# Two chained transformer blocks on one core: how the first unit starts, and four small orders in the second block

## The chip, the cores and the metric

The kernel runs on one core of a Trainium2 chip. The metric is the time of one execution on the device in microseconds (us); lower is better. The engines are TensorE (PE, with PEld for its weight loads), VectorE (DVE), ScalarE (ACT), GpSimd (POOL) and SyncE (SP), which here only issues DMAs.

## The reference

256 tokens of 1024 features go through a first block of two layers and then through a second block of two layers, all in float32. Cut to what matters here:

```python
def hybrid_layer(x, ...):            # first block, twice
    h = rms_norm(x, norm_mix_w)
    z = h @ w_in + b_in              # first unit: the first 512 columns
    ...                              # dilated attention, mLSTM, gates
    x = x + mixed @ w_out
    return x + jnp.square(relu(rms_norm(x, norm_mlp_w) @ w_ff1)) @ w_ff2

def first_block(x, ...):
    for l in range(2): x = hybrid_layer(x, ...)
    return rms_norm(x, final_norm_w)

def second_block(x, ...):            # again two layers
    for l in range(2):
        x = x + 0.5 * rmsnorm(swiglu_ffn(rmsnorm(x, pre_g), w_gu, w_down), post_g)
        x = x + rmsnorm(mixing_sublayer(rmsnorm(x, mix_pre_g), ...), mix_post_g)
        x = x + 0.5 * rmsnorm(swiglu_ffn(rmsnorm(x, pre2_g), w_gu2, w_down2), post2_g)
    return x
```

The mixing sublayer has four branches: a gated MLP, a pooling mixer, a sparse attention with a softmax, and a convolution of 31 taps.

## The kernel before

**Weights.** All weights come as chunks of 1 MB (128 partitions by 2048 floats, `CH` = 2048) in the order in which TensorE uses them, into three slots (`SLOTS` = 3). SP issues their DMAs, each after the slot's last low part is made (`lo_ready`). Each chunk is split: ScalarE writes `w_hi`, the chunk rounded to the matmul's format (`split_high`, L175), and VectorE writes `w_lo` = raw − `w_hi` (`split_low`, L182). The activations are split in the same way into `aH` and `aL`. A product is three matmuls: high·high, low·high, high·low. So TensorE does, for each chunk, one phase that needs `w_hi` and one that needs `w_lo` (for example L245 and then L251, or L327, L328 and then L335).

**Order.** Each engine runs a list in program order. `Splitter.upto(c)` puts the splits of all chunks up to `c` at that place of the list of ScalarE (`high`) or VectorE (`low`), so the lists interleave the splits with the rest of the work, written out by hand. Semaphores join the lists.

**The start (`first_block`).** SP issues: a head of constants with the identity (68 KB), token rows 0 to 127 (`x`, 512 KB), two halves of the first chunk, token rows 128 to 255, two halves of the second chunk, the third chunk. TensorE runs `WARM` = 4 matmuls on ones (L1313), transposes the first token tile (L1321), runs `FILL` = 3 matmuls on ones (L1360), then the first two products, and then the transposes of the second token tile. ScalarE and VectorE take the transposed tiles from the PSUM, times the norm's gain, into `aH` (`x_part_high`, L705) and `aL` (`x_part_low`, L931), and split the first two chunks in pieces (L719, L724, L726; L946, L959). `first_chunk` does the first unit of 512 columns with 48 matmuls, all of its products for one token tile before those for the other. Two `square_sum` (L411) on ScalarE give each token's sum of squares, from which VectorE makes `rstd`; the result is multiplied by it only when it is taken out of the PSUM (L994). GpSimd's list begins with two DMA issues, the broadcast rows `rows_a` (L617) and the constants (L619), once the second chunk has landed.

**The second block's start (layer 0).** VectorE multiplies each token tile by the final gain (L2366), then makes `first_v` and waits for its root from GpSimd. ScalarE squares the two new tiles (L2087), then makes the high part of chunk `F0[0] + 2`, the third that the feed-forward uses.

**`mlp`, four times.** VectorE makes the low parts of chunks 3 and 4 of the feed-forward one after the other, then `unit(1)` begins: the sum of halves of a (L262), its scaling (L2319), the sum of halves of b (L262 again), the low part of `lows[0]`, the product of both.

**The softmax, twice.** The rows of query tile 1 are normalised (L2532), then the low part of chunk `M0 + 17` is made, then query tile 0 is normalised (L2532). TensorE transposes the results (L2821, L2825).

Of the kernel before, what the change touches and what calls it, by code (L numbers as in the profile page):

```python
# [51 lines left out]
WARM, FILL = 4, 3  # L52
# [361 lines left out]
def token_rstd(k, dve, ch, layer, n):  # L414

    dve.wait_ge(k.ss_ready.sem, k.ss_ready.at(layer, TT * (n + 1)))
    dve.tensor_scalar(k.var[:, 0:TT], k.ss[:, 0:TT], 0.5 / DM, 0.5 * EPS, ALU.mult, ALU.add).then_inc(ch.sem, ch.one())
# [48 lines left out]
def first_block(nc, k, d, sems, block):  # L466

    with ExitStack() as ctx:
# [3 lines left out]
        def sig(name, per, start=0):  # L472
# [17 lines left out]
        R3 = sb("R3", [P, 8 * (SEQ + CONV - 1)])  # L490
        qk_tok = R1[:, 0:TT * 2 * AH * AD].rearrange("p (t h d) -> p t h d", t=TT, h=2 * AH)
# [59 lines left out]
        k.nT_done, k.aH_ready, k.a_ready = sig("nT_done", 8, 4), sig("aH_ready", 6, 4), sig("a_ready", 8, 4)  # L551
# [3 lines left out]
        x0_loaded, x1_loaded, half0_loaded, half1_loaded = (  # L555
            sig("x0_loaded", 0), sig("x1_loaded", 0), sig("half0_loaded", 0), sig("half1_loaded", 0))
        part_high, part_low = sig("part_high", 0), sig("part_low", 0)
        X_PARTS = tuple((tt, b) for tt in range(TT) for b in range(4))
        x_tile = lambda tt, kt: k.ps[:, ((4, 5, 6, 7), (2, 3, 4, 5))[tt][kt // 2], (kt % 2) * P:(kt % 2 + 1) * P]
# [55 lines left out]
        def _(pool):  # L615
            pool.wait_ge(k.raw_loaded[AHEAD_HIGH - 1], 16)
# [59 lines left out]
        def _(sp):  # L676
            sp.dma_start(consts[:, 0:KA_ADD], d.consts_a[:, 0:KA_ADD]).then_inc(head_loaded.sem, 16)
            sp.dma_start(k.x[:, 0, :], d.x[0:P, :]).then_inc(x0_loaded.sem, 16)
            sp.dma_start(k.raw[:, 0, 0:CH // 2], d.w_a[0, :, 0:CH // 2]).then_inc(half0_loaded.sem, 16)
            sp.dma_start(k.raw[:, 0, CH // 2:CH], d.w_a[0, :, CH // 2:CH]).then_inc(k.raw_loaded[0], 16)  # L680
            sp.dma_start(k.x[:, 1, :], d.x[P:2 * P, :]).then_inc(x1_loaded.sem, 16)
            sp.dma_start(k.raw[:, 1, 0:CH // 2], d.w_a[1, :, 0:CH // 2]).then_inc(half1_loaded.sem, 16)
# [11 lines left out]
        def _(act):  # L694
# [6 lines left out]
            def x_part_high(tt, b):  # L701

                act.wait_ge(k.nT_done.sem, 4 * tt + b + 1)
                for kt in (2 * b, 2 * b + 1):
                    ins = act.activation(k.aH[:, kt, tt * P:(tt + 1) * P], x_tile(tt, kt), ACT.Copy,  # L705
                                         scale=par[:, PA_NORM + kt:PA_NORM + kt + 1])
                ins.then_inc(k.aH_ready.sem, 1)

            def first_high():

                act.wait_ge(par0_loaded.sem, 16)
                for tt, b in X_PARTS[:2]:
                    x_part_high(tt, b)
                act.wait_ge(half0_loaded.sem, 16)
                for kt in range(4):
                    if kt == 2:
                        act.wait_ge(k.raw_loaded[0], 16)
                    cols = slice(kt * CH // 4, (kt + 1) * CH // 4)
                    act.activation(k.w_hi[0][:, cols], k.raw[:, 0, cols], ACT.Copy)\  # L719
                       .then_inc(part_high.sem if kt < 3 else k.hi_ready, 1)  # L720
                for tt, b in X_PARTS[2:]:
                    x_part_high(tt, b)
                act.wait_ge(half1_loaded.sem, 16)
                act.activation(k.w_hi[1][:, 0:CH // 2], k.raw[:, 1, 0:CH // 2], ACT.Copy).then_inc(part_high.sem, 1)  # L724
# [3 lines left out]
            for l in range(DEPTH):  # L728
# [7 lines left out]
                high.upto(2)  # L736
# [6 lines left out]
                if l == 0:  # L743
                    square_sum(k, act, l, 0, 0, junk)
                square_sum(k, act, l, 0, 1, junk)
# [144 lines left out]
        def _(dve):  # L890
# [6 lines left out]
            def angles(ch):  # L897

                dve.wait_ge(head_loaded.sem, 16)
# [26 lines left out]
            def x_part_low(tt, b):  # L926

                dve.wait_ge(k.aH_ready.sem, X_PARTS.index((tt, b)) + 1)
                for kt in (2 * b, 2 * b + 1):
                    cols = slice(tt * P, (tt + 1) * P)  # L930
                    ins = dve.scalar_tensor_tensor(k.aL[:, kt, cols], x_tile(tt, kt), par[:, PA_NORM + kt:PA_NORM + kt + 1],  # L931
                                                   k.aH[:, kt, cols].bitcast(F32), ALU.mult, ALU.subtract)
                ins.then_inc(k.a_ready.sem, 1)

            def first_low():

                dve.wait_ge(par0_loaded.sem, 16)
# [691 lines left out]
def second_block(nc, k, d, sems, block):  # L1629


    with ExitStack() as ctx:
# [581 lines left out]
        def _(dve):  # L2214
# [139 lines left out]
            for l in range(DEPTH):  # L2354
# [825 lines left out]
```

## Time and profile before

| | |
|---|---|
| median of 3 runs | 1792.0 us (1789.89 to 1793.45) |
| the profiled execution's own time | 1792.04 us |
| its span in the profile | 1790.3 us |
| mean granted clock of TensorE | 0.999 of full speed |

The span is the time between the first and the last recorded event of the core; some 1.7 us of the execution's time lie outside it. The profile comes from one execution. Its page gives busy times by engine; the timeline gives instructions by start and duration, neighbours of the same form in one row with a count (x8), and in brackets how long the engine had been idle and which event released it. A matmul of 512 columns is recorded with 0.38 us but such rows start 0.216 us apart, since matmuls are pipelined.

### The profile page before, as it was taken

To read this page: it belongs to the slowest core of one execution; us is meant where nothing else is said; L and a number is where in the kernel's file an instruction comes from. 1 tells how busy PE (TensorE), PEld (TensorE's weight loads), DVE (VectorE), ACT (ScalarE), POOL (GpSimd) and SP (SyncE) were. 2 spreads that over 40 slices of the span, in tenths; PEclk is the share of its full clock that TensorE was granted. 3 is DMA by queue.
4 is the path that set the end of the run, shared out by engine and by line. 5 is a ranking of instruction groups with operands and counts; after the bars stand their busy time and mean duration, and the time that the engine had idled before them with its cause. 6 is when DMAs were issued, how large, how long until landed. Compare 5 with 4: busy or idle time off the path is not lost.

```text
span 1790.3 us, 25922 instructions
## 1 busy us (share of the span) xinstructions
PE 1778.8 (99%) x10010; PEld 1588.6 (89%) x10010; DVE 1402.9 (78%) x1599; ACT 904.5 (51%) x998; POOL 219.7 (12%) x189
## 2 busy tenths in 40 slices
PE   9999999999999999999999999999999999999998
PEld 7988998889889898899898888998899898888997
DVE  7897867678869667777779987778777779987776
ACT  5564434445644444644555546444544555546443
POOL 0000000000001000000059230000000058230000
PEclk9999999999999999999999999999999999999999
DMA  9546565555556555655564556555655564555553
GB/s 315 205 157 227 188 212 209 189 215 200 187 215 222 205 196 186 214 197 194 181 204 172 183 210 217 202 196 192 223 199 197 188 203 167 186 212 205 201 197 117
DMA packets 52018, 357.43 MB, mean 200 GB/s; under 512 B 6552, under 2 KB 6688, under 8 KB 10080
## 3 DMA queue, kind: packets, MB, share of 16 engines
q1 hardware_dynamic: 47952, 341.93, 54.1%
q0 software_dynamic: 3696, 14.33, 2.7%
q8 instruction: 57, 0.93, 0.2%
q14 instruction: 25, 0.20, 0.0%
q10 hardware_dynamic: 288, 0.04, 0.0%
HBM read 354.15 MB, written 2.11 MB: 199 GB/s over the span
## 4 chain that ended last, share of the span: by engine, by line
PE 94%; DVE 4%; issue 1%; ACT 1%; DMA 1%; DVEq 0%; POOLq 0%; POOL 0%; SPq 0%; ACTq 0%
PE ps L245 21%; PE ps L327 13%; PE ps L335 13%; PE ps L328 13%; PE ps L251 11%; PE ps L207 3%; PE ps L208 3%; PE ps L209 3%; PE ps L225 2%; PE ps L232 2%; PE ps L226 2%; DVE w_lo L182 1%; PE ps L2917 1%; PE ps L2916 1%; PE ps L2921 1%
## 5 line engine op out<-in xcount | busy, mean ns | idle before, releaser
L182 DVE TENSOR_TENSOR w_lo<-raw,w_hi 128x2048 fp32r<-128x2048 f32 x312 | 717.4, 2305 | 208.4 <-ACT w_hi L175 208.0
L175 ACT ACTIVATE w_hi<-raw 128x2048 fp32r<-128x2048 f32 x312 | 596.1, 1912 | 424.1 <-PE ps L335 168.6
L245 PE MATMUL ps<-a,w_hi 128*128 128x512 f32 x1760 | 398.3, 379 | 0.8 <-ACT w_hi L175 0.8
L245 PEld LDWEIGHTS ps<-a,w_hi 128*128 128x128 f32 x1760 | 329.3, 189 | 46.0 <-ACT w_hi L175 1.2
L327 PE MATMUL ps<-w_hi,a 128*128 128x512 f32 x592 | 226.9, 383 | 0.0
L328 PE MATMUL ps<-w_hi,a 128*128 128x512 f32 x592 | 224.4, 379 | 0.0
L251 PEld LDWEIGHTS ps<-a,w_lo 128*128 128x128 f32 x1760 | 213.6, 192 | 5.9
L327 PE MATMUL ps<-w_hi,mix 128*128 128x512 f32 x576 | 218.7, 380 | 0.0
L328 PE MATMUL ps<-w_hi,mix 128*128 128x512 f32 x576 | 218.3, 379 | 0.0
L251 PE MATMUL ps<-a,w_lo 128*128 128x256 f32 x1760 | 214.2, 275 | 0.0
L335 PE MATMUL ps<-w_lo,a 128*128 128x512 f32 x592 | 139.8, 379 | 0.0
L335 PE MATMUL ps<-w_lo,mix 128*128 128x512 f32 x576 | 136.1, 379 | 0.0
L262 DVE TENSOR_REDUCE GU<-ps 128x512 f32<-128x1024 f32 x80 | 97.9, 1223 | 44.0 <-PE ps L251 44.0
L327 PEld LDWEIGHTS ps<-w_hi,a 128*128 128x128 f32 x592 | 111.9, 189 | 17.3 <-issue 1.4
L335 PEld LDWEIGHTS ps<-w_lo,a 128*128 128x128 f32 x592 | 111.9, 189 | 15.9
L328 PEld LDWEIGHTS ps<-w_hi,a 128*128 128x128 f32 x592 | 111.9, 189 | 15.1
L335 PEld LDWEIGHTS ps<-w_lo,mix 128*128 128x128 f32 x576 | 108.9, 189 | 15.4
L328 PEld LDWEIGHTS ps<-w_hi,mix 128*128 128x128 f32 x576 | 109.1, 189 | 13.7
L327 PEld LDWEIGHTS ps<-w_hi,mix 128*128 128x128 f32 x576 | 109.1, 189 | 13.6
L2041 ACT ACTIVATE GU<-GU 128x512 f32<-128x512 f32 x36 | 22.6, 629 | 176.1 <-DVE GU L2319 176.1
L1859 POOL TENSOR_TENSOR pss<-pss,neg_half 128x1 f32<-128x1 f32 x12 | 6.7, 558 | 690.8 <-DVE pss L2243 690.8
L225 PE MATMUL ps<-a,w_hi 128*128 128x256 f32 x320 | 73.2, 277 | 0.0
(416 smaller groups left out, 2267.2 us busy)
## 6 DMA issues: line engine op xcount, KB each, us to landing
raw<-in_w_b SPq DMA_DIRECT2D x198, 1024.0 KB, 4.9
raw<-in_w_a SPq DMA_DIRECT2D x124, 1024.0 KB, 4.9
rows<-in_post_gains POOLq DMA_DIRECT2D x6, 512.0 KB, 5.9
rows<-in_rows_a POOLq DMA_DIRECT2D x2, 1028.0 KB, 8.3
raw<-in_w_a SPq DMA_DIRECT2D x4, 512.0 KB, 7.1
rows<-in_rows_a POOLq DMA_DIRECT2D x2, 1024.0 KB, 6.9
x<-in_x SPq DMA_DIRECT2D x2, 512.0 KB, 6.0
a_gates<-bias_line POOLq DMA_DIRECT2D x2, 512.0 KB, 7.7
```

The costliest lines, as they stand in the source:

```text
L175: act.activation(k.w_hi[s], k.raw[:, s, :], ACT.Copy).then_inc(k.hi_ready, 1)
L182: dve.tensor_tensor(k.w_lo[s], k.raw[:, s, :], k.w_hi[s].bitcast(F32), ALU.subtract).then_inc(k.lo_ready, 1)
L207: pe.matmul(out, a[0], hi, start=first, stop=False)
L208: pe.matmul(out, a[0], lo, start=False, stop=False)
L209: return pe.matmul(out, a[1], hi, start=False, stop=end)
L225: pe.matmul(out, w, halves_in_turn(act(kt)[0]), start=n == 0 and kt == kts[0], stop=False)
L245: pe.matmul(both, hi[:, kt, n * P:(n + 1) * P], k.a[:, :, kt, :].rearrange("p s (t n) -> p s n t", t=TT), start=kt == 0, stop=False)
L251: end = pe.matmul(high, lo[:, kt, n * P:(n + 1) * P], halves_in_turn(k.aH[:, kt, :]), start=False, stop=kt == KT - 1)
L262: return dve.tensor_reduce(dst.rearrange("p f (t n) -> p f n t", t=TT), k.ps[:, bank:bank + 2, :].rearrange("p b (s n t) -> p b n t s", s= ...
L327: pe.matmul(in_pairs(out(tt, h)), a[0], w, start=first and i == 0, stop=False)
L328: pe.matmul(in_pairs(out(tt, h)), a[1], w, start=False, stop=False)
L335: ins = pe.matmul(in_pairs(out(tt, h)), act(kt)[0][:, tt * P:(tt + 1) * P], halves_in_turn(lo[:, i, h * step:(h + 1) * step]), start=False ...
```

## The change

1. **Tokens by features.** A new input `x_t` holds the tokens as features by tokens. SP loads it in four pieces of 256 KB between pieces of the first two chunks; it lies in `R1`. The 16 transposes, the two sets of `x_part_high` and `x_part_low` and `FILL` are gone, `WARM` is 8. ScalarE makes `aH` with `x_high(kt)` (256 columns from SBUF), interleaved with quarters of the chunks; VectorE makes `aL` with `x_low(kt)` (256 columns, both inputs in SBUF), interleaved with `quarter_low` and `next_low` (six pieces of 512 columns, one of 1024).
2. **Squares.** GpSimd squares each piece and adds it up, 15 operations of 128x256, ahead of its DMA issues. TensorE sums over the partitions with two matmuls by a column of ones after the first unit; `token_rstd` reads the PSUM. The two `square_sum` of layer 0 are gone.
3. **`first_chunk`** goes by `kt`: for both token tiles high·high, then low·high, then high·low, each after its own piece.
4. **Token rows** (`x`, 2 × 512 KB) are loaded by SP behind chunks 3 to 5; VectorE waits for them (`x_loaded`) ahead of the first residual that needs them.
5. **Second block, layer 0, start:** on ScalarE `high.upto(F0[0] + 2)` now stands ahead of the two squares; on VectorE `first_v` comes before the second gain multiply, and `low.upto(2)` before the wait for the root.
6. **`mlp`:** the low part of chunk 4 moves from behind that of chunk 3 to behind the sum of halves of b in `unit(1)`, in all four.
7. **Softmax:** the low part of chunk `M0 + 17` moves from between the two normalisations to behind both, in both layers.

```diff
-WARM, FILL = 4, 3
+WARM = 8
...
+            for kt in range(KT):
+                if kt == 0:
+                    pool.wait_ge(xT01_loaded.sem, 16)
...
+                if kt > 1:
+                    pool.wait_ge(squares.sem, 2 * kt - 1)
+                pool.tensor_tensor(xx[:, min(kt, 1), :], xT[:, kt, :], xT[:, kt, :], ALU.mult).then_inc(squares.sem, 1)
+                if kt > 0:
+                    pool.wait_ge(squares.sem, 2 * kt)
+                    pool.tensor_tensor(xx[:, 0, :], xx[:, 0, :], xx[:, 1, :], ALU.add).then_inc(squares.sem, 1)
             pool.wait_ge(k.raw_loaded[AHEAD_HIGH - 1], 16)
...
+            sp.dma_start(xT[:, 0:2, :], x_t[:, 0:2, :]).then_inc(xT01_loaded.sem, 16)
...
-            with sp.Fori(1, DEPTH * CA // SLOTS) as g:
+            for s in range(SLOTS):
+                sp.wait_ge(k.lo_ready, s + 1)
+                sp.dma_start(k.raw[:, s, :], d.w_a[SLOTS + s]).then_inc(k.raw_loaded[s], 16)
+            for tt in range(TT):
+                sp.dma_start(k.x[:, tt, :], d.x[tt * P:(tt + 1) * P, :]).then_inc(x_loaded.sem, 16)
+            with sp.Fori(2, DEPTH * CA // SLOTS) as g:
...
+            def x_low(kt):
+
+                dve.wait_ge(k.aH_ready.sem, kt + 1)
+                dve.scalar_tensor_tensor(k.aL[:, kt, :], xT[:, kt, :], par[:, PA_NORM + kt:PA_NORM + kt + 1],
+                                         k.aH[:, kt, :].bitcast(F32), ALU.mult, ALU.subtract).then_inc(k.a_ready.sem, 1)
...
+                x_low(0)
+                quarter_low(0)
...
+                x_low(6)
+                x_low(7)
+                next_low(2, CH // 2, CH)
...
+                for i in range(4):
+                    kt = 4 * half + i
...
+                    pe.wait_ge(k.aH_ready.sem, kt + 1)
...
+                            if half == 1:
+                                pe.wait_ge(squares.sem, 2 * KT - 1)
+                                for tt in range(TT):
+                                    ins = pe.matmul(k.ps[:, 6, tt:tt + 1], xx[:, 0, tt * P:(tt + 1) * P], ones[:, 0:1], start=True, stop=True)
+                                ins.then_inc(k.ss_ready.sem, TT)
...
                 if l == 0:
+                    high.upto(F0[0] + 2)
                     for tt in range(TT):
...
                 split_low(k, dve, st, l, F0[f] + 3)
-                split_low(k, dve, st, l, F0[f] + 4)
...
                     if j == 1:
+                        split_low(k, dve, st, l, F0[f] + 4)
                         split_low(k, dve, st, l, lows[0], trips)
...
                     dve.memset(v_tok[:, :, :, BD:BD + 1], 1.0).then_inc(vone_ready.sem, 1)
+                    low.upto(2)
                     dve.wait_ge(first_root.sem, 1)
...
                 for qt, cols in ((1, slice(P, 3 * P)), (0, slice(0, P))):
-                    if qt == 0:
-                        low.upto(M0 + 17)
...
                     dve.tensor_tensor(v, v, last(rsum[:, qt, :], (1 + qt) * P), ALU.mult).then_inc(p_ready.sem, 1)
+                low.upto(M0 + 17)
```

## Rows read from the trace of the kernel before

**Rows 1.** The page: busy time of each engine, its share of the span, instructions.

```profile
PE 1778.8 (99%) x10010; PEld 1588.6 (89%) x10010; DVE 1402.9 (78%) x1599; ACT 904.5 (51%) x998; POOL 219.7 (12%) x189
```

**Rows 2.** TensorE's waits: engine line waited for: total, times, longest.

```profile
PE ps L1321 <- DMA x<-in_x: 1.2, 1, 1.2
PE ps L2825 <- DVE RL L2532: 0.9, 1, 0.9
```

**Rows 3.** Timeline of TensorE, 0 to 33 us: start, duration, instruction, wait.

```profile
1.26 3.78 PE L1313 MATMUL ps<-ones 128*128 128x256 f32 x8 [1.26 <-DVE mv_tok L895]
...
7.15 1.46 PE L1360 MATMUL ps<-ones 128*128 128x256 f32 x6
9.37 0.45 PE L207 MATMUL ps<-w_hi,a 128*128 128x512 f32 x1 [0.75 <-DVE w_lo L946]
9.66 0.38 PE L208 MATMUL ps<-w_lo,a 128*128 128x512 f32 x1
...
20.93 0.38 PE L327 MATMUL ps<-w_hi,a 128*128 128x512 f32 x1
```

**Rows 4.** Timeline of VectorE, 8 to 26 us.

```profile
8.54 2.49 DVE L946 TENSOR_TENSOR w_lo<-raw,w_hi 128x512 fp32r<-128x512 f32 x4
...
14.30 2.36 DVE L959 TENSOR_TENSOR w_lo<-raw,w_hi 128x1024 fp32r<-128x1024 f32 x2 [0.17 <-ACT w_hi L724]
...
24.68 1.40 DVE L994 SCALAR_TENSOR_TENSOR R<-ps,rstd,rows 128x512 f32<-128x512 f32 x2
```

**Rows 5.** Windows: engines' busy us (instructions), clock, DMA share, GB/s.

```profile
2.00:4.00 2.00, 2.00 (x7) 1.56 (x6) 0.00 (x0) 1.23 (x2) 0.00 (x0) 1.00 0.90 202
4.00:6.00 2.00, 1.04 (x3) 0.32 (x1) 0.00 (x0) 0.00 (x0) 0.00 (x0) 1.00 1.03 346
```

**Rows 6.** Timeline of VectorE, 724 to 1011 us: forms alone, beside GpSimd.

```profile
724.72 4.49 DVE L182 TENSOR_TENSOR w_lo<-raw,w_hi 128x2048 fp32r<-128x2048 f32 x2 [0.50 <-ACT w_hi L175]
...
929.93 2.11 DVE L2439 SCALAR_TENSOR_TENSOR conv_y<-conv_x,rows,conv_y 128x256 f32<-128x256 f32 x4
...
983.59 4.04 DVE L2439 SCALAR_TENSOR_TENSOR conv_y<-conv_x,rows,conv_y 128x256 f32<-128x256 f32 x10
...
1005.71 5.39 DVE L182 TENSOR_TENSOR w_lo<-raw,w_hi 128x2048 fp32r<-128x2048 f32 x2
```

**Rows 7.** Timeline of GpSimd, 1004 to 1012 us.

```profile
1004.77 0.63 POOL L1916 TENSOR_TENSOR sum<-sum 128x265 f32<-128x265 f32 x1
...
1006.29 2.66 POOL L1916 TENSOR_TENSOR sum<-sum 128x257 f32<-128x257 f32 x1
1009.03 2.66 POOL L1930 TENSOR_TENSOR pooled<-sum,consts 64x256 f32<-64x256 f32 x1
```

**Rows 8.** The page's DMA issues: count, KB each, us from issue to landing.

```profile
rows<-in_rows_a POOLq DMA_DIRECT2D x2, 1028.0 KB, 8.3
```

**Rows 9.** Timeline of all engines, 717 to 721 us: the second block begins.

```profile
717.79 1.06 ACT L2087 ACTIVATE b_qkF<-x 128x1024 f32<-128x1024 f32 x1 [0.26 <-DVE x L2366]
...
718.84 1.89 ACT L175 ACTIVATE w_hi<-raw 128x2048 fp32r<-128x2048 f32 x1
...
720.79 3.72 PE L245 MATMUL ps<-a,w_hi 128*128 128x512 f32 x16 [0.79 <-ACT w_hi L175]
```

**Rows 10.** Timeline of all engines, 732 to 736 us: a feed-forward's second unit.

```profile
732.45 1.23 DVE L262 TENSOR_REDUCE GU<-ps 128x512 f32<-128x1024 f32 x1 [0.61 <-PE ps L251]
...
733.60 2.28 DVE L182 TENSOR_TENSOR w_lo<-raw,w_hi 128x2048 fp32r<-128x2048 f32 x1
...
735.71 1.46 PE L335 MATMUL ps<-w_lo,mix 128*128 128x512 f32 x6
```

**Rows 11.** Timeline of VectorE and TensorE, 978 to 984 us: the softmax's end.

```profile
978.81 3.36 DVE L182 TENSOR_TENSOR w_lo<-raw,w_hi 128x2048 fp32r<-128x2048 f32 x1
...
983.73 0.65 PE L2825 MATMUL ps<-consts,RL 128*128 128x128 f32 x4 [0.93 <-DVE RL L2532]
```

**Rows 12.** The chain of waits, 937 to 1017 us: start, us, what.

```profile
1015.95 1.16 PE ps L2844 x8
```

More of the change, by code:

```diff
@@ L411, in square_sum, with token_rstd @@
     act.activation(junk[:, tt, :], k.x[:, tt, :], ACT.Square, accum_out=k.ss[:, tt:tt + 1]).then_inc(k.ss_ready.sem, 1)
-def token_rstd(k, dve, ch, layer, n):
+def token_rstd(k, dve, ch, layer, n, sums=None):
     dve.wait_ge(k.ss_ready.sem, k.ss_ready.at(layer, TT * (n + 1)))
-    dve.tensor_scalar(k.var[:, 0:TT], k.ss[:, 0:TT], 0.5 / DM, 0.5 * EPS, ALU.mult, ALU.add).then_inc(ch.sem, ch.one())
+    dve.tensor_scalar(k.var[:, 0:TT], k.ss[:, 0:TT] if sums is None else sums, 0.5 / DM, 0.5 * EPS, ALU.mult, ALU.add).then_inc(ch.sem, ch.one())
     dve.wait_ge(ch.sem, ch.at(layer))
@@ L676, in _ @@
         def _(sp):
[L677 to L682 removed]
+            quarter = CH // 4
@@ L699, in _, with x_high @@
             act.activation(first_use[:, :], ones[:, 0:1], ACT.Copy)
[L701 to L707, printed above, removed]
+            def x_high(kt):
+                if kt < 2:
+                    act.wait_ge(xT01_loaded.sem, 16)
+                elif kt < 4:
+                    act.wait_ge(kt2_loaded.sem, 2 * 16)
+                elif kt < 6:
+                    act.wait_ge(half1_loaded.sem, 2 * 16)
+                else:
+                    act.wait_ge(head_loaded.sem, 2 * 16)
+                act.activation(k.aH[:, kt, :], xT[:, kt, :], ACT.Copy, scale=par[:, PA_NORM + kt:PA_NORM + kt + 1])\
+                   .then_inc(k.aH_ready.sem, 1)
@@ new lines, in quarter_high @@
+            def quarter_high(q):
+                if q == 0:
+                    act.wait_ge(quarter0_loaded.sem, 16)
+                elif q == 1:
+                    act.wait_ge(quarter1_loaded.sem, 16)
+                elif q == 2:
+                    act.wait_ge(kt2_loaded.sem, 2 * 16)
+                else:
+                    act.wait_ge(k.raw_loaded[0], 16)
+                cols = slice(q * CH // 4, (q + 1) * CH // 4)
+                act.activation(k.w_hi[0][:, cols], k.raw[:, 0, cols], ACT.Copy)\
+                   .then_inc(part_high.sem if q < 3 else k.hi_ready, 1)
@@ L709, in first_high @@
             def first_high():
                 act.wait_ge(par0_loaded.sem, 16)
[L712 to L724, printed above, removed]
+                x_high(0)
+                quarter_high(0)
+                x_high(1)
+                quarter_high(1)
+                x_high(2)
+                quarter_high(2)
+                x_high(3)
+                quarter_high(3)
+                x_high(4)
@@ L725, in first_high @@
+                act.activation(k.w_hi[1][:, 0:CH // 4], k.raw[:, 1, 0:CH // 4], ACT.Copy).then_inc(part_high.sem, 1)
+                x_high(5)
+                act.activation(k.w_hi[1][:, CH // 4:CH // 2], k.raw[:, 1, CH // 4:CH // 2], ACT.Copy).then_inc(part_high.sem, 1)
+                x_high(6)
+                x_high(7)
                 act.wait_ge(k.raw_loaded[1], 16)
@@ L735, in _ @@
                     high_of(k, act, l, 0, par[:, PA_NORM:PA_MLP], k.aH)
-                high.upto(2)
+                high.upto(3 if l == 0 else 2)
                 if l == 1:
@@ L1355, in x_next @@
                         ins.then_inc(qkT_done.sem, 1)
-            pe.wait_ge(head_loaded.sem, 16)
-            x_transpose(0)
-            for _ in range(FILL):
-                pe.matmul(k.ps[:, 1, 0:SEQ], ones[:, 0:P], ones[:, :], start=True, stop=True)
             for l in range(DEPTH):
```

144 lines of the change are left out of this document (79 added, 65 removed).

## The prediction

> **What bounds the kernel now.** I read the busy line of the page first: TensorE is busy 1778.8 of the span's 1790.3 us [rows 1]. So only TensorE's own waits can be won. Its list of waits names the places [rows 2]: 1.2 us for the first token tile and 0.9 us for the softmax's second normalisation, and the timeline has 0.79 at the second block's start [rows 9]. The timeline of the first microseconds adds what no list of waits shows: work that isn't the product. TensorE warms up from 1.26, runs fill at 7.15, starts the first product at 9.37 and the second unit at 20.93 [rows 3]. The mark for the prologue is that 20.93: behind it TensorE runs on the stream of chunks. A change anywhere else counts only if it moves the start of a matmul, so for each of the later edits I read the timeline of all engines around it.
>
> **Prologue, if nothing but TensorE bounds it.** Eight warm matmuls make 16 records. The first 8 took 3.78 us from 1.26; those at full pace took 1.46 for 6 [rows 3], of which the pace is 0.216, so 8 more take 1.7: warm ends at about 6.7. The first piece of tokens is by then in: the core's DMAs move 202 GB/s from 2 to 4 us and 346 from 4 to 6 [rows 5], so 256 KB land at about 4.2 and the next 256 KB, the first quarter of the chunk, at 4.9. The 48 matmuls at 0.216 take 10.37, the two sums over partitions 0.24: 17.35 instead of 20.93, a gain of 3.6. That is the case in which VectorE keeps up.
>
> **VectorE in the prologue.** The pieces of the low parts are priced by rows: 512 columns 0.60 each (2.49 for 4), 1024 columns 1.15 (2.36 for 2) [rows 4], 256 columns with both inputs in SBUF 0.40 (4.04 for 10) [rows 6]. Eight, six and one of them: 3.20 + 3.60 + 1.15 = 7.95 us. Alone they would follow ScalarE's pieces and end early enough.
>
> **GpSimd beside it.** GpSimd is at rest there before; now it runs 15 operations of 128x256, 14 of them beside VectorE's. What that costs is the largest unknown. Two low parts of 2048 columns take 4.49 us alone (at 724.72) and 5.39 (at 1005.71) beside GpSimd [rows 6], while GpSimd's operation of 128x257 takes 2.66 instead of the 0.63 of the like one at 1004.77 [rows 7]: it stands until VectorE's is through, and then VectorE's next one stands for it. The two alternate one by one: GpSimd's two stretched operations start 2.74 apart (1006.29 and 1009.03) [rows 7], and between them lies one low part, whose pace alone is 2.20 (4.49 less the last one's 2.29). So one GpSimd operation with two inputs costs VectorE 0.54. The bounds: below, nothing, as in the paragraph on TensorE, or the 0.2 that two GpSimd operations with one input each cost the four operations of 256 columns at 929.93 (2.11 where the ten at 983.59 give 4 × 0.40 and a tail of 0.07) [rows 6]; above, 0.68, a little over GpSimd's own 0.63 [rows 7], since its operation can't block for longer than it lasts with its start. The case in hand has two inputs and the same 256 columns, so I take 0.54: 14 × 0.54 = 7.56 us. VectorE starts with the first piece at 4.9 and ends its last at 4.9 + 7.95 + 7.56 = 20.4. Behind that piece stand 8 matmuls, 1.73, and the sums: 22.4 against 20.93, **+1.5 us**. With 0.2 each VectorE ends at 4.9 + 7.95 + 2.8 = 15.7 and TensorE at 17.6: −3.3, and −2.9 with some waits for pieces. With 0.68 each it ends at 22.4: +3.5.
>
> The row shows GpSimd's operation lengthened from 0.63 to 2.66 and VectorE's pair by 0.90. The Trainium skill, "SBUF — State Buffer", section "Who interferes with whom", says that the two share a port pair as an exclusive lock for a whole instruction, where VectorE has two SBUF inputs and GpSimd reads SBUF; PE and ACT have ports of their own. By that rule taken strictly each GpSimd operation costs its full length of 0.63: 14 × 0.63 is 8.8 us, 1.3 above the 7.56, and the prologue would lose 2.7 instead of 1.5. The trace agrees with the exclusive turns and shows a little less than the full length.
>
> **Transfers and what waits behind.** GpSimd issues the broadcast rows at about 19.4 to 21 instead of 13.12. They take 8.3 us to land [rows 8], so they are there at 27.7 to 29.3; VectorE takes the first unit out at 24.68 before [rows 4], then at 27.8 to 29.4 and is done 1.40 later. TensorE overwrites those banks with the third unit, 10.4 after the second's start, so at 32.8: 2 us are left, cost 0. The token rows' 1 MB delays the chunks behind it by at most the 3.0 us that 1 MB takes at 346 GB/s [rows 5]; three slots of chunks, 5.2 us of TensorE each, cover that: 0. ScalarE is freed of two square sums, which no matmul waited for: 0. The late wait for `x` stands near the end of the first layer: 0.
>
> **Second block's start.** TensorE's phase at 720.79 waited 0.79 for ScalarE's high part, made at 718.84 behind the second square at 717.79 [rows 9]; the lost time against the pace is 0.95. With the high part ahead of two squares of 1.06 it starts at about 716.4 and is ready at 718.3, and VectorE's low part, now ahead of the wait for the root, at 720.7: **−0.95**. The squares come 1.7 later, so `Silu` and the two high parts behind it by about 1.2; the first of those is then ready at 725.85, for a phase that would start 5.2 behind this one, at 726: nothing to spare, so −0.6 to −1.0.
>
> **Low part in `mlp`.** The sum of halves ends and the low part stands at 733.60, 2.28 long, so to 735.88; TensorE's low phase of chunk 4 starts at 735.71 [rows 10]. Before, chunk 4's low part was made at about 726.9, the second of the pair at 724.72 [rows 6], and the place at 733.60 held chunk 5's. Moved there it is seen by TensorE at about 735.94: 0.23 late, and a phase that had to stop starts with a step of 0.29 instead of 0.216, as 9.37 to 9.66 [rows 3]. 0.32 for each of the four feed-forwards (the other three show the same three rows, with the low phase 3.26 behind the sum in each): **+1.3** (0 to +1.4; VectorE idled 0.61 to 1.49 before that sum [rows 10], which may let it start sooner).
>
> **Low part in the softmax.** TensorE stands 0.93 at 983.73 for the second normalisation, which stood behind the low part of 3.36 at 978.81 [rows 11]. Moved behind, that wait goes, 1.1 with the restart. But the chain of waits from there to 1015.95 runs through VectorE [rows 12], whose work up to there is the same in sum; what TensorE gains at 983.73 it waits at L2844 for: **0** (−1.1 to +0.3). In layer 1 no wait stands there.
>
> **Sum.** +1.5 − 0.95 + 1.3 + 0 = +1.85 on the profiled execution's 1792.04, which is the median of the three runs (1792.0): **1793.9 us**. The bounds of the terms give 1792.04 − 3.6 − 1.0 + 0 − 1.1 = 1786.3 and 1792.04 + 3.5 − 0.6 + 1.4 + 0.3 = 1796.6.
>
> **Rivals.**
> 1. *GpSimd's squares stay off VectorE's way* (the cost is 0.2 or less). For: with one input the row shows so little [rows 6], and the operations have gaps between them, in which GpSimd waits for its own result. Against: the row with two inputs. Then −3.6 to −2.9 in the prologue: 1792.04 − 3.3 − 0.95 + 1.3 = 1789.1, and 1787.8 if the move in `mlp` is free too, 1786.7 if the softmax pays as well. Chance 0.32. One of those two extras is needed to get below 1788.4; I give that 0.55 of it.
> 2. *Slower: the broadcast rows come too late.* GpSimd's chain waits for data, for VectorE and for itself; if its last operation ends past 23.2, the rows land past 31.5 and VectorE empties the banks past 32.9. From that point each microsecond is one of TensorE's: an end at 27 (15 operations of 1.5) gives +3.8 more, 1797.7. For: GpSimd's operations beside VectorE took 2.66 each [rows 7]. Against: those stood behind low parts of 2.2, here behind 0.4 to 0.6. Chance 0.12.
> 3. *Slower: the clock.* Now TensorE waits for each piece, and the granted clock could fall; the rows at half pace took 0.43 for what takes 0.216 [rows 3]. Ten matmuls at that pace cost 2.2: 1796.1. Against: in 4 to 6 us, with 1.04 of 2.00 busy, the clock stays 1.00 [rows 5]. Chance 0.06.
> 4. *The softmax's move pays* the 1.1 us, with the rest as forecast: 1792.8; or the move in `mlp` costs nothing: 1792.6. Within the forecast's own range.
>
> **How the numbers follow.** The forecast has 0.50 and its own range 1791 to 1796. What a measurement of this kernel can tell from no change is 0.2%, 3.6 us: below 1788.4 is faster, above 1795.6 slower. Faster has 0.55 of rival 1, 0.18, and 0.02 of the forecast: 0.20. Slower has rivals 2 and 3 with 0.18, of which 0.03 stay inside and as much comes from the forecast's upper end: 0.18. The rest, 0.62, is the same. The range is 1786.7 to 1797: the first rival down to both extras and the upper bound of the terms; what is left out is most of rival 2 (0.1) and the tail below.
>
> **What would show it.** The second unit's first matmul at 22.4 (17.4 in rival 1). VectorE's pieces of 256 columns one by one at 0.9 to 1.0 of spacing, alternating with GpSimd's; GpSimd's 15 operations ending at 19 to 21. No wait at the phase at 720.79; a wait of 0.2 us at the low phase L335 in each feed-forward; no wait at L2825 but one of about 1 us at L2844. The prediction is wrong if VectorE's pieces keep their 0.4 and 0.6 us beside GpSimd, or if a new wait at the first evictions appears.

## The result and the profile after

The changed kernel takes 1794.12 us (median of 18 runs, 1792.88 to 1797.16) against 1791.43 us (18 runs, 1789.89 to 1793.45): a ratio of 1.0017 with the 95% interval 1.001 to 1.0024 (the medians themselves give 1.0015). That is 2.7 us slower, clear of no change, inside the 0.2% that were called the same (the interval's upper end is just outside), and 0.2 us from the forecast of 1793.9. The change itself was forecast at +1.85, from a profile of before that was 0.6 above the median of its 18 runs, so the two totals are closer than the two differences. The profiled execution of the changed kernel was its fastest, 1792.88 us with a span of 1791.2 us, so I took a second profile (experiment 1) before reading anything off the first.

TensorE's waits on the page of after: total, times, longest.

```profile
PE ps L1398 <- DVE w_lo L996: 2.0, 2, 1.6
PE ps L1387 <- ACT w_hi L768: 1.1, 1, 1.1
PE ps L1398 <- DVE w_lo L986: 0.3, 1, 0.3
```

They all lie in the prologue. The two of the second block [rows 2, 9, 11] are gone. TensorE in the prologue and at the three later places:

```profile
12.27 0.70 PE L1398 MATMUL ps<-w_lo,a 128*128 128x512 f32 x2 [0.33 <-DVE w_lo L986]
...
14.12 0.67 PE L1387 MATMUL ps<-w_hi,a 128*128 128x512 f32 x2 [1.15 <-ACT w_hi L768]
...
20.25 0.70 PE L1398 MATMUL ps<-w_lo,a 128*128 128x512 f32 x2 [1.62 <-DVE w_lo L996]
...
22.44 0.46 PE L327 MATMUL ps<-w_hi,a 128*128 128x512 f32 x1
...
721.87 3.62 PE L245 MATMUL ps<-a,w_hi 128*128 128x512 f32 x16
...
736.91 1.99 PE L335 MATMUL ps<-w_lo,mix 128*128 128x512 f32 x8
...
983.93 0.60 PE L2884 MATMUL ps<-consts,RL 128*128 128x128 f32 x4
...
1015.88 1.16 PE L2903 MATMUL ps<-consts,y 128*128 128x128 f32 x8
```

The second unit starts at 22.44 against 20.93 [rows 3]: +1.5, and 22.4 was forecast. The way there is another than the sum said. VectorE, its share of it:

```profile
5.50 0.79 DVE L976 SCALAR_TENSOR_TENSOR a<-R,a_par,a 128x256 fp32r<-128x256 f32 x1 [4.25 <-ACT a L739]
6.22 1.22 DVE L986 TENSOR_TENSOR w_lo<-raw,w_hi 128x512 fp32r<-128x512 f32 x1
...
13.49 0.48 DVE L976 SCALAR_TENSOR_TENSOR a<-R,a_par,a 128x256 fp32r<-128x256 f32 x1 [1.27 <-ACT a L739]
14.01 1.10 DVE L996 TENSOR_TENSOR w_lo<-raw,w_hi 128x512 fp32r<-128x512 f32 x1
15.04 0.83 DVE L976 SCALAR_TENSOR_TENSOR a<-R,a_par,a 128x256 fp32r<-128x256 f32 x1
15.79 1.22 DVE L996 TENSOR_TENSOR w_lo<-raw,w_hi 128x512 fp32r<-128x512 f32 x1
16.93 1.71 DVE L976 SCALAR_TENSOR_TENSOR a<-R,a_par,a 128x256 fp32r<-128x256 f32 x2
18.56 1.63 DVE L996 TENSOR_TENSOR w_lo<-raw,w_hi 128x1024 fp32r<-128x1024 f32 x1
```

GpSimd beside it, and the end of its chain:

```profile
15.66 0.80 POOL L631 TENSOR_TENSOR R<-R 128x256 f32<-128x256 f32 x1
16.61 0.88 POOL L628 TENSOR_TENSOR R<-R 128x256 f32<-128x256 f32 x1
...
19.19 1.59 POOL L631 TENSOR_TENSOR R<-R 128x256 f32<-128x256 f32 x1
20.73 0.74 POOL L633 DMA_DIRECT2D rows<-in_rows_a  x1
```

A piece of 256 columns that takes 0.40 alone is followed 0.75 later by the next (15.04 to 15.79), one of 512 columns 1.14 later (15.79 to 16.93) instead of 0.60. From 5.50 to the end of the last piece (the next instruction starts at 20.11) are 14.6 us, of which 1.27 is a gap ahead of 13.49; the pieces alone are 7.95, so GpSimd's 14 operations cost 5.4, 0.39 each, not 0.54 (0.41 if the one at 12.99, which ran in the gap, isn't counted). The gap and a start 0.6 late make up for it. The start: ScalarE's first piece waited for the constants with the norm's gain (`a_par`) until 4.96, and VectorE's stands 0.5 behind it, a step that the sum left out. The gap comes from the transfers, in the windows of after (busy times of PE, PEld, DVE, ACT, POOL; clock; share and GB/s of the DMAs) and in ScalarE's timeline:

```profile
4.00:6.00 2.00, 2.00 (x9) 1.69 (x8) 0.50 (x1) 1.00 (x2) 1.17 (x2) 1.00 0.97 277
6.00:8.00 2.00, 2.00 (x10) 1.54 (x9) 2.00 (x4) 1.31 (x4) 0.91 (x3) 1.00 1.02 355
8.00:10.00 2.00, 2.00 (x11) 1.70 (x9) 2.00 (x3) 1.84 (x4) 1.84 (x3) 1.00 1.00 252
18.00:20.00 2.00, 0.63 (x3) 0.20 (x2) 2.00 (x2) 1.48 (x2) 1.84 (x3) 1.00 0.08 33
```

```profile
12.95 0.51 ACT L739 ACTIVATE a<-R,a_par 128x256 fp32r<-128x256 f32 x1 [2.86 <-DMA raw<-in_w_a]
```

From 4 to 10 us the DMAs move 277, 355 and 252 GB/s, where before they moved 346 [rows 5] and then 379 and 410, and ScalarE starts on the fifth piece of tokens only at 12.95. What released it there is not the tokens. The kernel lets the fifth and sixth piece wait for two transfers with one semaphore (`half1_loaded`): the tokens, issued at 3.62 and landed 6.6 later, at 10.2, and the first half of the second chunk, issued at 4.14 and landed 8.8 later, at 12.9. With a semaphore of their own the two token pieces, and GpSimd's squares of them, could have run in the gap; no run tried it. TensorE's clock stays at 1.00.

**Where the time goes.** TensorE runs the same list in all kernels from the second unit on, so I matched its matmuls one by one and took, for each profile, the start of a matmul less its start in the profile of before. The offsets in us (the first column is the start of the second unit, the others stand just behind the places named; in the last column the end):

| profile | 20.9 | 120 | 719, ahead of the second block | 731 | 737, first low phase | 1017, behind the softmax | 1275 | 1560 | end |
|---|---|---|---|---|---|---|---|---|---|
| after | 1.51 | 2.03 | 2.03 | 0.98 | 1.30 | −0.07 | 0.60 | 0.50 | 0.83 |
| 1 after again | 1.65 | 4.22 | 4.21 | 3.15 | 3.48 | 3.01 | 3.67 | 4.57 | 4.89 |
| 2 prologue only | 1.25 | 2.47 | 2.47 | 2.45 | 2.45 | 1.22 | 1.22 | 2.10 | 2.10 |
| 3 second block only | −0.50 | −0.51 | −0.51 | −1.56 | −1.23 | −1.80 | −1.14 | −0.83 | −0.49 |
| 4 one square | −1.25 | 2.52 | 2.52 | 1.49 | 1.82 | 0.48 | 1.16 | 2.53 | 2.87 |
| 5 rows later | 1.16 | 1.24 | 1.24 | 0.21 | 0.54 | 0.51 | 1.19 | 1.22 | 1.56 |
| 6 rows later, one square | −1.39 | −1.10 | −1.10 | −2.14 | −1.81 | −2.33 | −1.65 | −0.18 | 0.17 |
| 7 low part 4 back | 1.13 | 1.49 | 1.49 | 0.46 | 1.64 | 0.57 | 0.60 | 0.95 | 0.96 |
| 8 orders, no low part 4 | −0.56 | −0.60 | −0.60 | −1.67 | −0.49 | −0.99 | −0.98 | −1.00 | −1.00 |
| 9 orders, first low part 4 | −0.70 | −0.71 | −0.71 | −1.78 | −1.46 | −2.85 | −2.85 | −2.52 | −2.52 |

Their ends agree with the executions' own times: 1792.04 + 0.83 = 1792.87 for 1792.88, 1792.04 + 4.89 = 1796.93 for 1796.94. Each row is one execution: that of 3 was the fastest of its 11 runs, those of 4 and 6 the slowest of theirs, so the last column isn't the medians' order.

### The profile page after: what moved, and what is told of

The parts are those of the page before. It is cut to its first block, busy times and chain, and to the rows that moved or that the text cites. A ratio compares the mean times of both kernels' runs of the same rounds, so it can differ in the third digit from the quotient of the medians.

```text
span 1791.2 us, 25902 instructions
## 1 busy us (share of the span) xinstructions
PE 1779.5 (99%) x10000; PEld 1587.3 (89%) x10000; DVE 1407.9 (79%) x1592; ACT 900.6 (50%) x987; POOL 229.9 (13%) x204
## 4 chain that ended last, share of the span: by engine, by line
PE 91%; DVE 5%; DMA 2%; issue 1%; POOL 0%; ACT 0%; SPq 0%; DVEq 0%; POOLq 0%
PE ps L245 21%; PE ps L335 13%; PE ps L327 13%; PE ps L328 13%; PE ps L251 11%; PE ps L207 3%; PE ps L209 3%; PE ps L208 3%; DVE w_lo L182 2%; PE ps L225 2%; PE ps L232 2%; PE ps L226 2%; DMA raw<-in_w_a 1%; PE ps L2975 1%; PE ps L2976 1%
## 5 line engine op out<-in xcount | busy, mean ns | idle before, releaser
L262 DVE TENSOR_REDUCE GU<-ps 128x512 f32<-128x1024 f32 x80 | 97.8, 1223 | 37.6 <-PE ps L251 37.6
```

The source lines that it names most:

```text
L262: return dve.tensor_reduce(dst.rearrange("p f (t n) -> p f n t", t=TT), k.ps[:, bank:bank + 2, :].rearrange("p b (s n t) -> p b n t s", s= ...
```

## The experiments

**1 to 4: the whole again, each half alone, and one square.** Experiment 1 is the changed kernel itself. Experiment 2 undoes the edits in the second block, experiment 3 makes them alone in the kernel before (both are the diffs shown ahead of the prediction, cut in two). Experiment 4 leaves out 14 of GpSimd's 15 operations:

```diff
-                if kt > 1:
-                    pool.wait_ge(squares.sem, 2 * kt - 1)
-                pool.tensor_tensor(xx[:, min(kt, 1), :], ...)
-                if kt > 0: ...                       # the sum
+                if kt == 0:
+                    pool.tensor_tensor(xx[:, 0, :], xT[:, kt, :], xT[:, kt, :], ALU.mult).then_inc(squares.sem, 1)
```

> The changed kernel once more, for a second profile. Its one profile is 0.9 us longer in span than that of before, its median over 18 runs 2.7 us above. If the profile is typical (theory A), the offset to before at the second unit is again +1.5 us and the end +0.7 to +0.9. If the rest is a transfer that lands at different times from run to run (theory B), this profile shows a larger offset, with another wait on a DMA in the first 60 us, and the end at +2 to +3.

> The changed start alone, the four orders of the second block as before. By the steps read in the profile of after: +1.5 at the second unit, +0.5 by 120 us, nothing behind: 1793.4 to 1794, about 2 above before. If the start costs what the median of the whole change shows (theory B), 3 to 4 above before, since the second block's edits gave back 1.2. If the start is no loss in most runs, within 1 us of before.

> The second block's orders alone, the start as before. By the offsets in the profile of after: -0.95 at the start of the block, four times +0.23 in the feed-forwards, -1.4 at the softmax: -1.2 to -1.4, so 1790.1. By the prediction's own terms (softmax 0, low part +1.3): +0.35, so 1791.8. Profile: no wait at L2825 and none at the phase behind it; if the softmax gave nothing, a wait of 1 us stands at the matmuls on y (L2844 of before).

> The changed kernel with GpSimd making one square and none of the other 14 operations; the sum of squares is left out of the result but for the first eighth of the features. If GpSimd's operations beside VectorE's are what costs (theory C), VectorE's pieces take 0.40, 0.60 and 1.15 again and the last ends about 14.5 to 16; the second unit starts at 17.4 to 18.5 and the time is 4 us below the changed kernel's, 1790. If the late pieces by DMA are what costs (rival: the fifth piece of tokens landed at 12.95), the second unit starts no earlier than 20: from 12.95 on come 24 matmuls, 5.2 us, plus VectorE's pieces: 18.4 to 20, and the time falls by 2 to 3.

Before in these runs: 1791.42. Experiment 1: 1794.39 us, ratio 1.0018 (1.0009 to 1.0027). Its profile ends at +4.89, past both theories (+0.7 to +0.9 and +2 to +3): the first one wasn't typical, and the two differ between 21 and 120 us, as theory B says. Its waits:

```profile
PE ps L1398 <- DVE w_lo L996: 2.0, 2, 1.6
PE ps L1387 <- ACT w_hi L768: 1.0, 1, 1.0
PE ps L1543 <- DVE R L1209: 0.9, 1, 0.9
PE ps L2903 <- DVE consts L2621: 0.7, 2, 0.4
PE ps L327 <- ACT w_hi L175: 0.4, 1, 0.4
```

The prologue is the same; new is a loss of 2.6 between 21 and 120 us, a wait of 0.4 for a chunk's high part and one of 0.9 for VectorE's work on the attention, which comes late. Experiment 2: 1793.64, ratio 1.0013 (1.0004 to 1.0022), +2.2, near what the first theory gave. Experiment 3: 1792.4, ratio 1.0006 (0.9997 to 1.0015), +1.0, where the offsets of after said −1.3 and the prediction's own terms +0.35; the interval (−0.5 to +2.7) holds the second, not the first. The two halves add up to the whole, 2.2 + 1.0 for 3.0.

Experiment 4: 1792.68, ratio 1.0006 (0.9997 to 1.0015), which is 1.7 below experiment 1 and not the 4 of theory C. VectorE's pieces are back at their own pace:

```profile
13.02 0.48 DVE L972 SCALAR_TENSOR_TENSOR a<-R,a_par,a 128x256 fp32r<-128x256 f32 x1 [2.43 <-ACT a L735]
13.54 0.69 DVE L992 TENSOR_TENSOR w_lo<-raw,w_hi 128x512 fp32r<-128x512 f32 x1
14.15 0.48 DVE L972 SCALAR_TENSOR_TENSOR a<-R,a_par,a 128x256 fp32r<-128x256 f32 x1
...
16.20 1.23 DVE L992 TENSOR_TENSOR w_lo<-raw,w_hi 128x1024 fp32r<-128x1024 f32 x1 [0.18 <-ACT w_hi L770]
```

The second unit starts at 19.68, so GpSimd's operations cost 2.8 us of TensorE's time. But that is not the 17.35 of the unbound case: ScalarE starts on the fifth piece at 12.48 still, TensorE goes on with the second chunk at 13.65, and its 24 matmuls from there take 5.2. And the gain is lost again: −1.25 at 20.9 becomes +2.52 by 120 us. That made the late token rows the suspect.

**5 and 6: token rows out of the way.** SP loads them behind chunk 14 instead of behind chunk 5; in experiment 6 with one square only as well.

```diff
-            for s in range(SLOTS):
-                sp.wait_ge(k.lo_ready, s + 1)
-                sp.dma_start(k.raw[:, s, :], d.w_a[SLOTS + s]).then_inc(k.raw_loaded[s], 16)
+            for c in range(SLOTS, 5 * SLOTS):
+                sp.wait_ge(k.lo_ready, c - SLOTS + 1)
+                sp.dma_start(k.raw[:, c % SLOTS, :], d.w_a[c]).then_inc(k.raw_loaded[c % SLOTS], 16)
...
-            with sp.Fori(2, DEPTH * CA // SLOTS) as g:
+            with sp.Fori(5, DEPTH * CA // SLOTS) as g:
```

> The changed kernel with the two loads of token rows moved behind chunk 14 (about 80 us) instead of behind chunk 5. Theory A: the megabyte, issued at 23.3 with GpSimd's megabyte of broadcast rows at 20.7, is what delays the chunks (ScalarE's third chunk behind it ran at 40.8 instead of 33.0) and makes TensorE wait at 43 and the chain to 120 us late. Then the offset at 20.93 stays +1.5, at 43 it stays +1.5 to +1.7, at 120 us +1.5 to +2.0, and the median falls by 1 to 2, to 1792.5 to 1793.4. Rival: it is GpSimd's late issue (rows and the gates' bias line behind it) alone that makes the chain late; then the offset at 120 us stays 2.5 to 4 and the median within 0.5 of the changed kernel's.

> As the run before, and GpSimd makes one square and none of the other 14 operations; the sum of squares is left out of the result but for the first eighth of the features. With both costs gone the second unit starts 1.2 earlier than before, as with one square alone, and by theory A nothing of it is lost by 120 us (with one square alone it was: -1.25 became +2.5). Then -1.2 -0.95 -0.5 +0.9: 1789.5 to 1790.5. If the offset at 120 us is again above +1.5, the loss between 20 and 120 us isn't due to the token rows, and the median stays at 1792.5.

Before in these runs: 1791.69. Experiment 5: 1793.01, ratio 1.0006 (0.9997 to 1.0015); experiment 6: 1790.9, ratio 0.9995 (0.9986 to 1.0004). Experiment 6 is 0.4 above the range expected of it. Between 20.9 and 120 us they lose 0.1 and 0.3; the profiles with the rows behind chunk 5 lost 0.4 to 2.6, and the one with one square 3.8. Each of those has a step of 0.2 to 1.3 at 43.5 us, where TensorE waits for the high part of the chunk behind chunk 6 (the 0.4 in the list of experiment 1); experiments 5 and 6 have none there. ScalarE's split of chunk 6 in after and then in experiment 5:

```profile
33.80 1.92 ACT L175 ACTIVATE w_hi<-raw 128x2048 fp32r<-128x2048 f32 x1 [6.63 <-DMA raw<-in_w_a]
40.76 0.63 ACT L598 ACTIVATE w_hi<-raw 128x512 fp32r<-128x512 f32 x1 [5.04 <-DMA raw<-in_w_a]
```

```profile
33.30 1.91 ACT L175 ACTIVATE w_hi<-raw 128x2048 fp32r<-128x2048 f32 x1 [6.63 <-DMA raw<-in_w_a]
36.84 0.63 ACT L598 ACTIVATE w_hi<-raw 128x512 fp32r<-128x512 f32 x1 [1.64 <-DMA raw<-in_w_a]
```

It is 7.8 us later in after than in before, where it ran at 32.98, and 3.9 later without the rows. The issues of the first 60 us of after say why:

```profile
rows<-in_rows_a POOLq DMA_DIRECT2D x1, 1028.0 KB, 9.7
x<-in_x SPq DMA_DIRECT2D x2, 512.0 KB, 12.3
```

The token rows take 12.3 us to land, since GpSimd's two late issues (20.7 and 21.5 us, 1.4 MB) are under way with them, and chunk 6 stands behind both. Theory A holds by the matched steps; the medians alone wouldn't show it, since the intervals of the changed kernel and of experiment 5 overlap. GpSimd's late issue alone (the rival) leaves the split 3.9 us late, and there 0.1 is lost.

**7 to 9: the low part of chunk 4.** Experiment 7 is the changed kernel without that move. Experiment 8 is the kernel before with the other two orders and without it, experiment 9 with the move in the first feed-forward alone:

```diff
                 split_low(k, dve, st, l, F0[f] + 3)
-                split_low(k, dve, st, l, F0[f] + 4)
+                if (l, f) != (0, 0):
+                    split_low(k, dve, st, l, F0[f] + 4)
...
                     if j == 1:
+                        if (l, f) == (0, 0):
+                            split_low(k, dve, st, l, F0[f] + 4)
```

> The changed kernel with the low part of chunk 4 back behind that of chunk 3 in the four feed-forwards. Each of them showed a step of 0.22 to 0.33 at the low phase: 0.9 less in sum, 1793.3. The prediction's size was 1.3: 1792.9. If VectorE's later sum of halves costs as much in return, no change: 1794.2.

> The kernel before with the new orders at the second block's start and in the softmax, without the move in the feed-forward. By the offsets in the profile of the second block's edits alone: -0.95 at the start, -1.1 at the softmax, +0.5 at the matmuls on y, +0.4 in layer 1: -1.1, 1790.3. By the profile of after (-1.4 at the softmax, nothing in layer 1): -2.3, 1789.1. By the prediction's terms (softmax 0): -0.95, 1790.5. If the run with all of the second block's edits, 1.0 above before, had its loss in the softmax rather than in the feed-forward: 1791.5 or more.

> The kernel before with the new orders at the second block's start and in the softmax, and the low part of chunk 4 moved in the first feed-forward alone. The run without that move lost 0.9 us at 732 us (TensorE waited 0.8 for VectorE's sum of halves); the run with it in all four lost 0.22 to 0.34 at each low phase. Moved in the first alone, it should lose 0.22 once: 0.7 below the run without, three times 0.25 below the run with all four: offset -0.5 at the start, -1.45 at 720, -1.2 at 736, -1.6 at the end, 1790.2, 1.2 below before. Rival: the wait for the sum of halves comes from the new start itself and only moves to the next phase; then the time stays at 1790.9.

Experiment 7: 1793.6, ratio 1.0014 (1.0005 to 1.0023); experiment 8: 1790.89, ratio 0.9996 (0.9987 to 1.0005). Both show what the prediction didn't see. In the first feed-forward of experiment 8:

```profile
725.11 4.50 DVE L182 TENSOR_TENSOR w_lo<-raw,w_hi 128x2048 fp32r<-128x2048 f32 x2 [1.38 <-ACT w_hi L175]
729.52 0.69 DVE L2346 TENSOR_TENSOR mix<-ps,mix 128x512 fp32r<-128x512 f32 x1
730.12 1.22 DVE L262 TENSOR_REDUCE GU<-ps 128x512 f32<-128x1024 f32 x1
```

```profile
731.59 0.45 PE L327 MATMUL ps<-w_hi,mix 128*128 128x512 f32 x1 [0.84 <-DVE GU L262]
```

With ScalarE's squares moved back everything behind them is late: the pair of low parts starts at 725.11 instead of 724.72 [rows 6], while TensorE is 1.7 us ahead. The pair holds VectorE until 729.6, and TensorE's next phase waits 0.84 for the sum of halves L262, which ends at 731.3, and starts at 731.59. The offset goes from −1.67 to −0.49: all that the new start had won. With the low part moved, the sum comes first and that loss of 1.18 becomes 0.32; the other three feed-forwards pay 0.33 each with nothing in return. Experiment 9 says so: 1790.12 us (1790.2 was expected) against 1791.63, ratio 0.9992 (0.9983 to 1.0001), 1.5 below and the best kernel of the study, though its interval still touches no change; its profile loses 0.32 at the first and nothing at the other three, and of its waits

```profile
PE ps L1321 <- DMA x<-in_x: 0.3, 1, 0.3
PE ps L2850 <- DVE consts L2568: 0.2, 1, 0.2
```

only these two are left behind the warm-up. It was not timed beside experiment 8, so the 0.8 between their medians rests on the offsets.

**10 to 12: two attempts at a better prologue, both worse.** Experiment 10 takes the squares from GpSimd: the token rows are loaded right behind chunk 2 and ScalarE squares them again, the low part 4 as in experiment 9. In the kernel before the squares stood ahead of chunk 3's high part (17.11 and 19.19); here they stand behind it. Experiment 11 has in addition larger pieces (tokens by features in 2, the first chunk in 2); experiment 12 is the changed kernel with the larger pieces alone.

```diff
             sp.dma_start(k.raw[:, 2, :], d.w_a[2]).then_inc(k.raw_loaded[2], 16)
+            for tt in range(TT):
+                sp.dma_start(k.x[:, tt, :], d.x[tt * P:(tt + 1) * P, :]).then_inc(x_loaded.sem, 16)
...
+                if l == 0:                                   # behind high.upto(3)
+                    act.wait_ge(x_loaded.sem, 2 * 16)
+                    act.wait_ge(k.a_ready.sem, KT)
+                    square_sum(k, act, l, 0, 0, junk)
...
-            sp.dma_start(xT[:, 0:2, :], x_t[:, 0:2, :]).then_inc(xT01_loaded.sem, 16)
-            sp.dma_start(k.raw[:, 0, 0:quarter], ...)            # and six more
+            sp.dma_start(xT[:, 0:4, :], x_t[:, 0:4, :]).then_inc(xT01_loaded.sem, 16)
+            sp.dma_start(k.raw[:, 0, 0:CH // 2], ...)            # and three more
```

> The changed kernel without GpSimd's squares: the token rows are loaded ahead of chunk 3 and ScalarE squares them as before; the low part of chunk 4 moves in the first feed-forward alone. With one square alone the second unit started at 19.5 to 19.7; so here, 1.3 before the kernel before. If the rows (1 MB, ahead of chunk 3, in a stretch where the queue stood nearly empty from 18 to 22 us) cost nothing there, the offset at 120 us is -1.3 to -0.8 and the end at -2.5: 1789. If they delay chunk 3, TensorE waits for ScalarE's high part at the third unit, 1 to 2 us, and the time is 1790 to 1791.

> As the run before, with the tokens by features in two pieces of 512 KB and the first chunk in two halves, instead of eight pieces of 256 KB. The small pieces moved 252 to 277 GB/s where the halves of before moved 346 to 410. If the size of the rows of a piece is the cause, the fifth piece lands at about 10 instead of 12.5, TensorE doesn't wait at 13 and the second unit starts at 17.4 to 18.5: another 1.2 to 2 less, 1787.5. If the rate is set by the start of all queues rather than by the pieces, the first matmul comes 1 us later, at 8, and the second unit at 19.5 to 20: no gain, 1789 to 1790.

> The changed kernel with the larger pieces alone; GpSimd's squares stay. If its operations beside VectorE's bound the prologue by themselves (0.4 to 0.5 us for each of 14), the second unit starts no earlier than 21: VectorE's first piece at 6, 7.95 of its own and 5.6 to 7.6 of GpSimd's, then 8 matmuls and the sums: 21.5 to 23.5, and the median stays at 1794. If the late fifth piece is what adds, the gap of 1.3 us in VectorE's work at 12 us goes and the second unit comes at 20.9 to 21.2: 1792.8.

Before in these runs: 1791.63. Experiment 10: 1798.53, ratio 1.0034 (1.0022 to 1.0047), where 1789, or 1790 to 1791 with a late chunk 3, was expected. The second unit starts 1.49 before that of before, and then:

```profile
PE ps L335 <- DVE w_lo L182: 3.0, 1, 3.0
PE ps L327 <- ACT w_hi L175: 2.4, 1, 2.4
```

```profile
25.20 1.91 ACT L175 ACTIVATE w_hi<-raw 128x2048 fp32r<-128x2048 f32 x1 [6.02 <-DMA raw<-in_w_a]
27.02 1.04 ACT L411 ACTIVATE R<-x 128x1024 f32<-128x1024 f32 x1
...
29.23 0.17 DVE L417 TENSOR_SCALAR var<-ss 128x2 f32<-128x2 f32 x1 [7.72 <-ACT R L411]
...
31.58 2.29 DVE L182 TENSOR_TENSOR w_lo<-raw,w_hi 128x2048 fp32r<-128x2048 f32 x1
```

ScalarE gets chunk 3 at 25.20, where it had it at 19.61 in experiment 4, and TensorE wants it at 24.6. The queue that stood empty at 18 to 22 us did so behind chunk 3; a megabyte ahead of that chunk pushes it into the empty stretch and past its end: 5.6 us later, with GpSimd's 1.4 MB (issued at 15.1 and 15.8) under way beside it. That is the wait of 2.4. The wait of 3.0 comes from the order. The token rows had landed by 20.4, but ScalarE's list has their squares behind chunk 3's high part, at 27.02; VectorE makes `rstd` from them ahead of chunk 3's low part, so it stood 7.72 us and made that low part at 31.58. With the squares ahead, as in the kernel before, VectorE could have made it from 27.1 to 29.4, and TensorE wanted it at 30.9. That is an estimate from these rows; no run has that order, so the two experiments don't show that the idea itself is bad. Experiment 11: 1796.06, ratio 1.0024 (1.0014 to 1.0033), where 1787.5 to 1790 was expected: the same two waits, with 1.2 instead of 2.4 for the high part; its second unit starts at 18.8, 2.1 before that of before. Experiment 12: 1797.03, ratio 1.0029 (1.0017 to 1.004), 3 above the 1794 expected: second unit at 23.15, +2.2 instead of +1.5 and inside the expected 21.5 to 23.5; in its profile 1.1 more is lost by 120 us and 2.5 between 1275 and 1560 us (point 6 below). So without GpSimd's operations the larger pieces help by 0.6, and beside them they cost 0.7: VectorE's first piece starts at 6.43 instead of 5.50, its second has to wait for the first chunk's half. Experiment 12 gives the cleanest price, since VectorE has no gap from 8.18 on:

```profile
8.96 0.95 DVE L960 SCALAR_TENSOR_TENSOR a<-R,a_par,a 128x256 fp32r<-128x256 f32 x1
9.84 1.10 DVE L970 TENSOR_TENSOR w_lo<-raw,w_hi 128x512 fp32r<-128x512 f32 x1
...
18.43 1.34 DVE L960 SCALAR_TENSOR_TENSOR a<-R,a_par,a 128x256 fp32r<-128x256 f32 x2
```

Five pairs of a 256- and a 512-column piece take 9.47 us, 1.89 each (8.96 to 18.43) instead of 0.40 + 0.60, with two GpSimd operations to the pair: 0.45 for each.

## Why the prediction was right, and where it was not

1. *Prologue, +1.5.* Measured +1.51, +1.65, +1.25, +1.13 and +1.16 in five profiles. The cause was named rightly: without the operations 2.8 us less (experiment 4). The term behind it was mis-sized: 0.39 for each GpSimd operation, and 0.45 where VectorE has no gap (experiment 12), not 0.54, so 5.4 us for 14 and not 7.56; and the sum had VectorE start at 4.9 and never wait, where it started at 5.50 and stood 1.27 for the second chunk's first half. Two errors of 2 us cancelled, so that the 22.4 came out to the tenth is luck. The sign named for it missed too: VectorE's pieces of 256 columns were spaced 0.71 to 0.82 beside GpSimd's, not 0.9 to 1.0. Rival 1's condition wasn't met, and with it met (experiments 4 and 6) the start gave −1.25 and −1.39, not −3.6, since the second chunk's first half landed at 12.5 there as well. Rival 2 didn't come: GpSimd's chain ended at 20.8, short of 23.2. The rows took 9.7 us and not 8.3, so VectorE took the first unit out at 30.44, past the forecast 27.8 to 29.4, and was done at 31.8, 1.1 ahead of TensorE and not 2; the cost of 0 held. Rival 3 neither: the clock stayed at 1.00.
2. *"Three slots of chunks cover that: 0."* This is the step that failed. The token rows cost 0.4 to 2.6 between 21 and 120 us in four profiles and 0.1 with the rows later; by the medians 1.1 to 1.4 (1794.12 and 1794.39 against 1793.01). The delay was bounded by 3.0 us, 1 MB at 346 GB/s, where chunk 6 came 7.8 later: 3.9 for the token rows, and 3.9 from GpSimd's 1.4 MB, which the change itself puts into the same microseconds and which the sum left out. With the rows later 11 runs spread over 2.6 us, with the changed kernel in the same number 5.2.
3. *Second block's start, −0.95.* Measured −0.92 to −0.97 at the matmul of 720.79 in each of the nine profiles that have it, and another 0.1 behind it. But "nothing to spare" behind it was too kind: without the move of low part 4, 1.18 is lost at 732 (experiments 7 and 8). The prediction priced that move against the order of before alone, and so not the wait that it takes away.
4. *Low part in `mlp`, +1.3.* Measured 0.32, 0.33, 0.34, 0.33 in after: 1.32, as each step was priced. But undoing the move doesn't give 1.32 back: in the first feed-forward 1.18 is lost instead of 0.32, so the offsets give three times 0.33 less 0.86, 0.1 in all. The median of experiment 7 is 0.5 to 0.8 below the whole change's, within the width of the intervals.
5. *Softmax, 0.* The stall of 983.73 went (−1.1), and the wait that was to take its place came in part: from 737 to 1017 us the offset changed by −0.03 to −1.39 in the nine profiles of the table that have the edit, −0.8 in the mean. So 0 was the upper end, not the likeliest, for the stretch. In experiment 2, without the edit and with TensorE 2.45 late, the same stretch gave back 1.23: the same −1.09 stands at 983.73 as with the edit, so a late TensorE doesn't meet the stall, and the edit is worth nothing beside a slow prologue. Only with the prologue of before (experiments 3, 8 and 9: −0.57, −0.50 and −1.39) can the gain be the edit's.
6. *What stays open.* Between 1275 and 1560 us the offset moved by −0.1 to +1.5 in the ten profiles of the table, 0.5 in the mean, and in experiment 2, without the softmax edit, by 0.9. Whether the edit has a share in it isn't settled: one profile of each kernel isn't enough, and there is one of before.

In sum, against the profile of before: +1.3 (the mean of point 1) + 1.2 (token rows, the mean of four) − 1.0 + 1.3 − 0.8 + 0.5 (point 6) = 2.5. The profile of before was itself 0.6 above the median of its 18 runs; experiments 3, 8 and 9, which have its prologue, start the second unit 0.5 to 0.7 earlier, since TensorE waits 0.3 to 0.5 for the first token tile there and 1.2 in that profile [rows 2]. So the sum against the median is 3.1, where 2.7 and 3.0 were measured. The forecast had +1.85 by other terms: the token rows' 1.2 and the late 0.5 were missing, the softmax stretch's −0.8 too, and 0.6 lay in the profile it started from.

## What to carry to other kernels

An operation moved to an idle engine isn't free when its operations and those of the busiest engine take turns, as here: price it by a row in which the two run side by side, at the size of the pieces at hand. Where a change delays one transfer and adds another, put both on one line of time with everything issued in those microseconds, and ask which chunk stands behind them. And price an edit of order against the kernel as it will be with the other edits: here the new start gave 1.0 us only because the low part had moved out of its way, and that move was needed in one feed-forward of four. When work is moved back to an engine, put it where it stood: in experiment 10 the squares behind one more high part held VectorE for 7.7 us.

## What was not expected of the hardware

GpSimd's and VectorE's operations of like length, 0.4 to 0.7 us, took turns as the long ones did [rows 6, 7], but each GpSimd operation cost VectorE 0.39 to 0.45 instead of 0.54. The Trainium skill, "SBUF — State Buffer", section "Who interferes with whom", has the whole operation blocked, which by GpSimd's 0.61 (its operation at 12.99, when VectorE stood still) would be 0.61 each; the traces show two thirds to three quarters of that.

Halving a transfer from rows of 4 KB to rows of 2 KB for each partition went with 277, 355 and 252 GB/s instead of 346, 379 and 410 from 4 to 10 us. The first half of the second chunk, with about 2 MB ahead of it in both, landed at 12.9 instead of 11.1. Experiment 11 against 10 puts 0.6 us of the second unit's start on it. No run separates the size of the rows from the number of transfers in flight.
